# Two gate projections of each merge tile moved ahead of the projections of the attention outputs

## The reference, cut to what matters

```python
for l in range(DEPTH):
    h = rms_norm(x, norm_g[l])
    proj = jnp.einsum('btd,dc->btc', h, w_in[l])
    q_a, kv_a, g_a, z_a, q_b, k_b, v_b, f_b, z_b, merge = jnp.split(proj, split_at, axis=-1)
    y_a = nsa_mixer(...) * jax.nn.silu(z_a)
    y_b = fox_mixer(...) * jax.nn.silu(z_b)
    r_a, r_b = jnp.split(merge, 2, axis=-1)
    merged = (jax.nn.sigmoid(r_a) * jnp.einsum('btc,cd->btd', y_a, w_proj_nsa[l])
              + jax.nn.sigmoid(r_b) * jnp.einsum('btc,cd->btd', y_b, w_proj_fox[l]))
    x = x + jnp.einsum('btd,de->bte', merged, w_out[l])
return rms_norm(x, final_g)
```

## Time and profile before

| what | us |
|---|---|
| median of 3 runs | 1598.87 (1598.45 to 1600.92) |
| the profiled execution | 1599.08 |
| its span in the profile | 1597.3 |
| TensorE busy | 1528.7 (96%) |
| VectorE busy | 956.7 (60%) |
| ScalarE busy | 923.3 (58%) |
| GpSimd busy | 465.7 (29%) |

### The profile page before, as it was taken

The page is one execution under the profiler, slowest core; times in us unless marked ns, Lnnn a source line. Parts: engine busy times, 40 slices in busy tenths (PEclk is TensorE's granted clock), DMA queues, the critical chain, the costliest instruction groups (busy, mean ns, idle before and its releaser), DMA issues.

```text
span 1597.3 us, 26922 instructions
## 1 busy us (share of the span) xinstructions
PE 1528.7 (96%) x7664; PEld 1254.7 (79%) x7664; DVE 956.7 (60%) x2298; ACT 923.3 (58%) x1905; POOL 465.7 (29%) x586
## 2 busy tenths in 40 slices
PE   4999999999999989999969999999999999899996
PEld 2778888888888878888748788888888888688885
DVE  6376776776676763333365666776776676533344
ACT  3377777777777752222246777777777776422222
POOL 3144354354354320000013354354354353000000
PEclk8999999999999999999979999999999999999998
DMA  8232222222222233333532222222221221333331
GB/s 204 68 82 54 54 54 53 54 54 54 53 53 53 54 97 102 92 99 97 137 99 66 68 55 54 53 53 54 54 53 53 53 54 51 121 92 101 96 94 64
DMA packets 224384, 117.96 MB, mean 74 GB/s; under 512 B 20640, under 2 KB 221344, under 8 KB 223776
## 3 DMA queue, kind: packets, MB, share of 16 engines
q1 hardware_dynamic: 219104, 107.66, 25.2%
q0 software_dynamic: 1728, 8.66, 1.4%
q10 hardware_dynamic: 3456, 0.54, 0.2%
HBM read 110.41 MB, written 6.42 MB: 73 GB/s over the span
## 4 chain that ended last, share of the span: by engine, by line
PE 90%; issue 3%; DVE 3%; ACT 2%; POOL 1%; ACTq 1%; DMA 0%; DVEq 0%; POOLq 0%
PE acc L1353 63%; PE o_pair L1431 8%; PE turned L1413 7%; PE scores L1404 4%; PE scores L1405 4%; PE o_pair L1458 2%; PE turned L1510 1%; PE misc L1442 1%; DVE h_raw L1009 1%; DVE rstd L1001 1%; ACT kk_hi L746 0%; PE misc L1376 0%; PE misc L1450 0%; POOL q_swap L531 0%; ACT q_swap L709 0%
## 5 line engine op out<-in xcount | busy, mean ns | idle before, releaser
L1353 PE MATMUL acc<-h_hi,w_hi 128*128 128x512 f32 (+1 forms) x1152 | 455.9, 396 | 27.0 <-DVE h_lo L397 24.4
L1353 PE MATMUL acc<-h_hi,w_lo 128*128 128x512 f32 (+1 forms) x1152 | 454.1, 394 | 0.0
L1353 PE MATMUL acc<-h_lo,w_hi 128*128 128x512 f32 (+1 forms) x1152 | 453.5, 394 | 0.0
L981 DVE TENSOR_TENSOR w_lo<-w_raw,w_hi 128x1024 fp32r<-128x1024 f32 x192 | 235.2, 1225 | 153.8 <-ACT w_hi L673 151.2
L803 ACT ACTIVATE prob<-prob,row_max 128x128 f32<-128x128 f32 (+3 forms) x384 | 214.5, 559 | 127.4 <-DVE row_max L1099 125.0
L673 ACT ACTIVATE w_hi<-w_raw 128x1024 fp32r<-128x1024 f32 x192 | 200.6, 1045 | 143.8 <-PE acc L1353 138.8
L1353 PEld LDWEIGHTS acc<-h_hi,w_hi 128*128 128x128 f32 (+1 forms) x1152 | 215.6, 187 | 74.7 <-DVE h_lo L397 29.7
L596 POOL TENSOR_SCALAR prob<-prob,row_inv,gates 128x128 f32<-128x128 f32 (+3 forms) x256 | 156.4, 611 | 356.9 <-DVE row_inv L1106 356.3
L1099 DVE CUSTOM_DVE_ANT_0 prob<-scores,causal 128x128 f32<-128x128 f32 (+3 forms) x384 | 185.4, 483 | 117.2 <-PE scores L1405 109.9
L1353 PEld LDWEIGHTS acc<-h_hi,w_lo 128*128 128x128 f32 (+1 forms) x1152 | 215.5, 187 | 43.0
L1353 PEld LDWEIGHTS acc<-h_lo,w_hi 128*128 128x128 f32 (+1 forms) x1152 | 215.7, 187 | 41.8
(11 more groups left out here) (163 smaller groups left out, 2168.8 us busy)
## 6 DMA issues: line engine op xcount, KB each, us to landing
w_raw<-in_w_in_dram SPq DMA_DIRECT2D x140, 512.0 KB, 3.8
w_raw<-in_w_proj_nsa_dram SPq DMA_DIRECT2D x16, 512.0 KB, 3.5
w_raw<-in_w_proj_fox_dram SPq DMA_DIRECT2D x16, 512.0 KB, 3.6
w_raw<-in_w_out_dram SPq DMA_DIRECT2D x16, 512.0 KB, 3.5
x_scratch<-xT POOLq DMA_DIRECT2D x2, 2048.0 KB, 9.3
xT<-x_scratch POOLq DMA_DIRECT2D x2, 2048.0 KB, 8.4
x_nat<-in_x_dram SPq DMA_DIRECT2D x2, 1024.0 KB, 6.8
c_w<-in_cmp_w_k_dram SPq DMA_DIRECT2D x4, 512.0 KB, 7.6
```

The costliest lines, as they stand in the source:

```text
L981: dve.tensor_tensor(w_lo[:, par, :, 0:width], w_raw[:, par, :, 0:width], w_hi[:, par, :, 0:width], ALU.subtract).then_inc(w_lo_done, 1)
L1353: ins = pe.matmul(acc[par][0:width, :], w[:, par, k, 0:width], rhs, start=(n == 0), stop=(n == 23))
```

## The change

TensorE's order in the merge becomes: gates of tile 1, projections of tile 0, then for e = 2 to 7 the gates of e and the projections of e - 1, and at the end the projections of tile 7. SP's loads are put in the same order. The tanh tiles get a second buffer (`m_th` is [P, 2, 2, T], indexed by e % 2), and `yt_hi` and `yt_lo` become two tiles per mixer so that `m_th` lies where keys of the first mixer were. The first tanh of tile 0 moves into the last attention cycle, the second stands ahead of the wait for `y_mul`. The high and low parts of the second mixer's outputs are made in two portions with weight splits between them. The loops of ScalarE and VectorE over e are written out; TensorE's stays a loop.

```diff
-            yt_hi = sb("yt_hi", [P, 2, KT, T], F32R)
-            yt_lo = sb("yt_lo", [P, 2, KT, T], F32R)
-            m_th = sb("m_th", [P, 2, T])
+            yt_hi = [sb("yt_hi0", [P, KT, T], F32R), sb("yt_hi1", [P, KT, T], F32R)]
+            yt_lo = [sb("yt_lo0", [P, KT, T], F32R)]
+            m_th = sb("m_th", [P, 2, 2, T])
+            yt_lo.append(sb("yt_lo1", [P, KT, T], F32R))
...
-                with sp.Fori(0, KT) as e:
-                    half = base + U_MERGE // 2 + 2 * e
+                merge0 = base + U_MERGE // 2
+                load(w_view, l, C_RA, P, merge0, 0)
+                load(w_view, l, C_RB, P, merge0, 1)
+                with sp.Fori(1, KT) as e:
+                    half = merge0 + 2 * e - 1
                     load(w_view, l, C_RA + P * e, P, half, 0)
                     load(w_view, l, C_RB + P * e, P, half, 1)
-                    load(wn_view, l, P * e, P, half + 1, 0)
-                    load(wf_view, l, P * e, P, half + 1, 1)
+                    load(wn_view, l, P * e - P, P, half + 1, 0)
+                    load(wf_view, l, P * e - P, P, half + 1, 1)
+                load(wn_view, l, P * (KT - 1), P, merge0 + 2 * KT - 1, 0)
+                load(wf_view, l, P * (KT - 1), P, merge0 + 2 * KT - 1, 1)
...
                 if cycle.last:
                     at(CYCLE_STEPS, lambda: lower_half(fox, 0))
                     at(CYCLE_STEPS + LAG_PV, lambda: lower_half(fox, 1))
+                    at(plan.end[4] + 2, lambda: gate_tanh(cycle.unit(4)[0], 0, 0))
...
+                gate_tanh(merge0, 0, 1)
+                split_hi(merge0 + 1, 1)
+                act.wait_ge(y_mul, 2 * PAIRS * (l + 1) + 2)
+                yt_high(0, (0, 2, 4, 6))
+                split_hi(merge0 + 2, 0)
+                gate_tanh(merge0 + 1, 1, 0)
+                yt_high(1, (0, 2))
+                split_hi(merge0 + 2, 1)
+                gate_tanh(merge0 + 1, 1, 1)
+                yt_high(1, (4, 6))
+                split_hi(merge0 + 3, 0)
+                merged_high(0)
+                for e in range(2, KT):
+                    half = merge0 + 2 * e - 1
+                    split_hi(half, 1)
+                    gate_tanh(half, e, 0)
+                    split_hi(half + 1, 0)
+                    gate_tanh(half, e, 1)
+                    split_hi(half + 1, 1)
                     split_hi(half + 2, 0)
+                    merged_high(e - 1)
...
+                split_lo(merge0 + 1, 1)
+                yt_low(0, (0, 2, 4, 6))
+                split_lo(merge0 + 2, 0)
+                yt_low(1, (0, 2))
+                split_lo(merge0 + 2, 1)
+                yt_low(1, (4, 6))
+                for e in range(KT):
+                    half = merge0 + 2 * e + 2 if e < KT - 1 else merge0 + 2 * KT - 1
+                    part(half, e, 0)
                     split_lo(half + 1, 0)
+                    part(half, e, 1)
+                    merged(e)
+                    if e < KT - 1:
+                        split_lo(half + 1, 1)
+                    if e < KT - 2:
+                        split_lo(half + 2, 0)
+                        split_lo(half + 2, 1)
...
+                for n in range(2):
+                    unit_piece(0, 24, merge0 + 1, n, free=(m_th_done, base + n + 1))
+                for n in range(2):
+                    projected(merge0 + 2, n, (m_th_done, base + 2 + n + 1),
+                              each_k=lambda k: (yt_lo_done, KT * l + KT // 2 * n + k // 2 + 1))
+                with pe.Fori(2, KT) as e:
+                    half = merge0 + 2 * e - 1
                     for n in range(2):
+                        unit_piece(0, 24, half, n, free=(m_part, base + 2 * e + n - 1))
+                    for n in range(2):
+                        projected(half + 1, n, (m_th_done, base + 2 * e + n + 1))
+                for n in range(2):
+                    projected(merge0 + 2 * KT - 1, n, (m_part, base + 2 * KT + n - 1))
```

More of the change, by code:

```diff
@@ L765, in z_tanh_of, with gate_tanh @@
                 act.activation(z_silu[:, b, :], acc[par][:, :], ACT.Tanh, scale=0.5).then_inc(z_th_done, 1)
+            def gate_tanh(half, e, par):
+                act.wait_ge(unit_mm, 2 * half + par + 1)
+                act.activation(m_th[:, e % 2, par, :], acc[par][:, :], ACT.Tanh, scale=0.5)\
+                    .then_inc(m_th_done, 1)
             def body(cycle):
@@ L925, in _ @@
                 cycles(act, l, body)
[L927 to L932, removed]
-                    split_hi(half + 2, 0)
-                    act.wait_ge(m_sum_done, KT * l + e + 1)
-                    act.activation(m_hi[:, bass.ds(e, 1), :], m_sum[:, 0:1, :], ACT.Copy, scale=0.5)\
-                        .then_inc(m_hi_done, 1)
@@ L939, in _ @@
[L939 to L955, removed]
+                merge0 = half0 + U_MERGE // 2
+                def yt_high(mixer, pieces):
+                    for k in pieces:
+                        act.activation(yt_hi[mixer][:, k:k + 2, :], y_all[mixer][:, k:k + 2, :],
+                                       ACT.Copy).then_inc(yt_hi_done, 1)
@@ new lines, in merged_high @@
+                def merged_high(e):
+                    act.wait_ge(m_sum_done, KT * l + e + 1)
+                    act.activation(m_hi[:, e:e + 1, :], m_sum[:, 0:1, :], ACT.Copy, scale=0.5)\
+                        .then_inc(m_hi_done, 1)
+                gate_tanh(merge0, 0, 1)
[4 more added lines that the diff above has]
+                gate_tanh(merge0 + 1, 1, 0)
@@ L956, in _ @@
+                split_hi(merge0 + 2 * KT - 1, 1)
+                split_hi(merge0 + 2 * KT, 0)
+                merged_high(KT - 1)
                 out0 = half0 + U_OUT // 2
@@ L1261, in _, with yt_low, part, merged @@
                 cycles(dve, l, body)
-                for mixer in range(2):
-                    for k in range(0, KT, 2):
+                merge0 = half0 + U_MERGE // 2
+                def yt_low(mixer, pieces):
+                    for k in pieces:
                         dve.wait_ge(yt_hi_done, KT * l + KT // 2 * mixer + k // 2 + 1)
[L1266 to L1279, removed]
+                        dve.tensor_tensor(yt_lo[mixer][:, k:k + 2, :], y_all[mixer][:, k:k + 2, :],
+                                          yt_hi[mixer][:, k:k + 2, :], ALU.subtract).then_inc(yt_lo_done, 1)
+                def part(half, e, n):
+                    if e:
+                        dve.wait_ge(m_lo_done, KT * l + e)
+                    dve.wait_ge(m_th_done, 2 * KT * l + 2 * e + n + 1)
+                    dve.wait_ge(unit_mm, 2 * half + n + 1)
+                    dve.scalar_tensor_tensor(m_sum[:, n, :], m_th[:, e % 2, n, :], 1.0, acc[n][:, :],
+                                             ALU.add, ALU.mult).then_inc(m_part, 1)
+                def merged(e):
                     dve.wait_ge(m_part, 2 * KT * l + 2 * e + 4)
@@ L1282, in merge_sums @@
                     dve.wait_ge(m_hi_done, KT * l + e + 1)
-                    dve.scalar_tensor_tensor(m_lo[:, bass.ds(e, 1), :], m_sum[:, 0:1, :], 0.5,
-                                             m_hi[:, bass.ds(e, 1), :], ALU.mult, ALU.subtract
+                    dve.scalar_tensor_tensor(m_lo[:, e:e + 1, :], m_sum[:, 0:1, :], 0.5,
+                                             m_hi[:, e:e + 1, :], ALU.mult, ALU.subtract
                                              ).then_inc(m_lo_done, 1)
[L1287 to L1290, removed]
-                    split_lo(half + 1, 0)
-                    split_lo(half + 1, 1)
-                    merge_sums(half, e)
+                split_lo(merge0 + 1, 1)
[7 more added lines that the diff above has]
+                    part(half, e, 0)
+                    split_lo(half + 1, 0)
+                    part(half, e, 1)
[5 more added lines that the diff above has]
+                        split_lo(half + 2, 1)
                 def residual(j, par):
@@ L1548, in _, with projected @@
                 cycles(pe, l, body)
[L1550 to L1555, removed]
-                    for n in range(2):
[L1557 to L1560, removed]
+                merge0, base = half0 + U_MERGE // 2, 2 * KT * l
+                def projected(half, mixer, free, each_k=None):
+                    unit_piece(0, 24, half, mixer, hi=yt_hi[mixer], lo=yt_lo[mixer], each_k=each_k, free=free)
+                for n in range(2):
[5 more added lines that the diff above has]
+                    half = merge0 + 2 * e - 1
+                    for n in range(2):
+                        unit_piece(0, 24, half, n, free=(m_part, base + 2 * e + n - 1))
[3 more added lines that the diff above has]
+                    projected(merge0 + 2 * KT - 1, n, (m_part, base + 2 * KT + n - 1))
                 def out_unit(j, par, each_k=None):
```

## The result

The changed kernel takes 1582.76 us (median of 4 runs, 1582.54 to 1583.47) against 1599.65 us (4 runs, 1598.45 to 1600.92): ratio 0.9895, 95% interval 0.9878 to 0.9912, so 1.0% faster. The forecast was 1584.2 with a range of 1582.0 to 1588.4. The profiled execution took 1582.94 us, 16.1 less than the 1599.08 of before.

The account below looks back on a forecast made before the run. TensorE, busy 96% of the span, was taken as the bound. Terms 11.8 + 4.5 - 1.0 - 0.4 = 14.9 us, off the profiled 1599.08, gave 1584.2 us, range 1582.0 to 1588.4.

Parts of the forecast that it names:

- The idle gap: TensorE's wait after the last value product: filled by tile 1's gate units, saving 5.9 us a layer, 11.8 in all.
- the clock: TensorE behind the gap: without it the clock has no reason to fall to 0.50, saving 1.65 + 2.83 = 4.5 us.
- The early tanh: Tile 0's first tanh, moved into ScalarE's idle stretch in the last attention cycle: its 0.60 us is hidden, costing nothing.
- Rival 2: Wait returns at tile 0's projection through late outputs or early tanh; tanh behind `o_low` costs 1.3 us a layer, 1586.8; chance 0.06.
- The load: Weights of (merge0 + 2, par 1), now beside the reload of x: landing 594.0 to 594.5, 0.5 us a layer, -1.0 us.
- the second gate unit: Merge start: tile 1's second gate unit starts at 585.8, its low split from VectorE ready at 583.9, 1.9 us early.
- Rival 1: Weight load starts only after the reload of x: landing 596.8, TensorE waits 2.5 us a layer, 1588.2; chance 0.14.
- Steady rounds: Merge rounds after the start: the tight link keeps its chain with 1.0 us to spare; cost none.
- written-out loops: ScalarE and VectorE read about seven times the merge's instructions in a line; between nothing and 4.78 us, taken as nothing.
- Rival 4: Code loading stalls each written-out merge round by 4.78 us, 3.8 over the margin, 14 rounds: +53, about 1637; chance 0.03.
- Seams: TensorE's change from cycle to merge code, and the clock at the second layer's first units: -0.4 us together.
- the gross gain: Both layers' merges: closed gap and kept clock together save 16.3 us, before the costs are taken off.

Follow-up runs that it names:

- The filler: Kernel before, plus 24 useless TensorE matmuls between the last value product and the first projection: 1595.36 us, ratio 0.9980.
- the tanh experiments: Changed kernel with tile 0's first tanh directly behind `o_low`: 1585.84 us; with both tanhs and the weight split behind the wait for `y_mul`: 1595.92 us.
- the run with its loop: Changed kernel with ScalarE's merge code for tiles 2 to 7 as a loop of three turns of two tiles: 1583.06 us, ratio 0.9897.
- The run with the wait: Changed kernel with VectorE's low split of (merge0 + 1, par 1) held until GpSimd's last product of `y_all` is done: 1583.96 us, one run.

## Why the prediction was right, point by point

- **The idle gap, 11.8 us, and the clock, 4.5 us.** Right. The merges are 7.17 and 8.94 us shorter; forecast before the load were 5.92 + 1.65 = 7.57 and 5.92 + 2.83 = 8.75. The filler shows the clock's part by itself (4.0 us), the tanh experiments show the idle part opening again, 1.4 and 3.7 us a layer, as priced.
- **The early tanh costs nothing.** Right: it runs at 575.43, in the idle stretch of the earlier trace rows, and `o_low` starts 0.02 us behind the value product as before. Rival 2, that the tanh would be bound behind `o_low`, did not happen; built by hand it came to 1585.84, where that rival's steps gave 1.3 us a layer.
- **The load, -1.0 us.** The place and the limit were right, the size too large, and that the landing came out inside the forecast 594.0 to 594.5 was in part luck. It landed 9.9 us after its issue, at 594.4, against a limit of 594.3: the first layer waits 0.2 us, and its merge is 0.54 us over the undisturbed 206.75. In the second layer it took 9.2 us and met its limit. So the term measures 0.5, not 1.0. Three errors inside it partly cancelled. It was issued at 584.5, not at 583.9, since the split ahead of it took 1.76 us, which the step "the second gate unit" had at 1.23. Beside the reload far less of it got through than the 150 to 300 packets of the sum. These are the queues of the changed kernel from 584.4 to 590.5 us, and from 591.0 to 594.5 (columns as in the earlier trace rows):

```profile
q0 software_dynamic: 119, 1.95, 84.5%
q1 hardware_dynamic: 40, 0.02, 1.1%
...
q1 hardware_dynamic: 1929, 0.97, 103.9%
```

  Until 588.5 not one packet of q1 passed; from then to 590.5 it was 40 beside 50 of q0. And the reload had moved all but some 0.02 MB of its 2.10 MB by 591.0, earlier than the 592.5 of the sum, but the load then needed 3.4 us and not 1.5 to 2, with the next load behind it on the same queue. The row that the rate was taken from, mixes two things: up to 803.0 us q1 has 50 packets beside 49 of q0, one for one, and the other 87 of its 137 pass in the last half microsecond.
- **Rival 1, the load held back wholly.** Its picture of the queues was nearer to the traces than the forecast's share. What it had wrong is the time at which the load gets its turn: 591, when the bytes of the reload are through, not 593.8, when its landing is reported. Enforced by a wait, the load landed at 596.8, as that rival has it; TensorE waited 2.1 and 1.5 us, not 2.5, and by the lengths of the merges it cost 5.3 us against the changed kernel, 1.7 of them for the clock, which fell once. The rule that the prediction cites from the Trainium skill (page "DMA: Bandwidth & Descriptors", section "Queues, rings and completion order"), that an SDMA engine drains a packet of some 9 to 17 descriptors before it switches to another queue, gives the direction: turns of equal length, for descriptors of 512 bytes and of 16 KB, would let about as many of the one pass as of the other, as from 588.5 on. That none passed in the 3 us before is not explained by it (without the reload the load's packets start 0.9 us after its issue, here 4 us), and what held them there stays open.
- **Steady rounds and written-out loops, nothing.** Right, and shown for ScalarE by the run with its loop. Rival 4 had the price of a stall right, 4.5 us of time for 4.8 to 5 us of issue, but such a stall comes with the jump back and not with straight code.
- **Seams, -0.4 us.** Too much by about its size. The turn of the loop took 5.12 instead of 4.78 us, the second layer's first units 25.27 instead of 25.34, and the attention cycles of the second layer came out 0.4 shorter. Together 0.1 in favour of the change.
- **Sum.** Forecast 14.9, measured 16.1 by the profiled executions; by the medians 16.9, and 14.4 when the changed kernel was measured again. The terms above are told apart by the profiles, not by the medians. The missing 1.2 are, within 0.2, the load (0.5), the seams (0.5) and the gross gain (16.3, where the two merges at 206.75 us save 16.65).
- **An error in a sign that I gave.** The prediction said that 40 units would run from the last value product on and take 217.6 us. The change only reorders: 38 units, 206.75 us. The sum did not use the 40.

## What to carry to other kernels

When the engine that sets the time waits for a chain on other engines, look for work of its own that is already fed, and then check what frees its buffers: here the reader of one bank had to move as well, or the new order was worth 2.6 us instead of about 16. Price such a gap twice, once as idle and once at the clock behind it. And after moving work forward, look which transfers it releases earlier and beside what: the load that was free in its old place ended 0.1 us past its limit in the new one.

## What the runs showed of the hardware

- **Gaps and TensorE's clock.** After two waits of 1.4 us the granted clock stayed at 1.00. After 2.1 us it fell to 0.50 once, though TensorE was already at work again, and after 1.5 us it did not. After 3.7 and 5.9 us it fell each time, four of four. The loss was 1.65 us (half of 3.31) to 2.8 us (half of 5.65) each time.
- **VectorE beside GpSimd.** A subtraction with both operands in SBUF took 1.76 instead of 1.22 us beside GpSimd's product, 0.54 more, of 0.69 us in which the two overlapped. The Trainium skill has it, page "SBUF — State Buffer", section "Who interferes with whom": such an instruction contends with a GpSimd instruction that reads SBUF, and the second to come is held until the first is done. By that it would have ended at 583.33 + 1.22 = 584.55; it ended at 584.40, so the trace agrees to 0.15 us. The run with the wait agrees too: starting 0.8 us later cost only 0.3 us at the end.
- **A small transfer beside a large one.** 512 KB took 9.2 and 9.9 us beside a 2 MB transfer of another queue, and 3.6 us without it. With packets of 512 bytes against 16 KB, none of the small ones passed for the first 3.5 us of the large transfer's packets, then about one for one of the large; all but 77 of some 1000 waited until the large one's bytes were through. The large one took 8.8 us, 0.1 more than in the earlier trace rows.
- **A loop's long jump back.** 4.7 us on ScalarE and 5.0 us on VectorE in the changed kernel (4.0 to 5.2 and 4.6 to 5.9 in the kernels of this study that jump back), each once, at the turn from the first layer to the second, and 4.5 us of the kernel's time. Two packets of a queue of kind instruction pass in that pause, and none where the jump is gone.
